# First w_up tile split into high and low parts at the 96th exponential and scaling of the attention instead of the 48th

## What is computed

```python
o_nsa = nsa_attention(...)            # 8 heads, blocks: compressed, selected, window
o_fox = forgetting_attention(...)     # 8 heads, causal with decay
merged = sigmoid(gm_nsa) * (o_nsa @ w_up_nsa) + sigmoid(gm_fox) * (o_fox @ w_up_fox)
return merged @ w_o
```

## Time and profile before

| | |
|---|---|
| time, median of 3 runs | 2453.43 us (2452.48 to 2454.91) |
| profiled execution, its own time | 2450.02 us |
| its span in the trace | 2448.1 us |
| PE busy | 95% of the span |
| DVE, ACT, POOL busy | 57%, 44%, 51% |
| granted TensorE clock, mean | 0.98 of full speed |

### The profile page before, as it was taken

How to read it: one execution, slowest core, us unless ns; L and a number is a source line. 1 busy time by engine, 2 the same in 40 slices (tenths; PEclk the granted TensorE clock), 3 DMA queues, 4 the chain that set the end, 5 groups by cost and what they waited for, 6 DMA issues and landing times. The chain is left out here.

```text
span 2448.1 us, 30080 instructions
## 1 busy us (share of the span) xinstructions
PE 2316.3 (95%) x10920; PEld 1884.8 (77%) x10920; DVE 1385.6 (57%) x1664; ACT 1088.6 (44%) x2060; POOL 1249.8 (51%) x967
## 2 busy tenths in 40 slices
PE   4999999999999899999799999999789999999997
PEld 2788888888877777788677877777578888888885
DVE  5846555266557755742588888575463323225554
ACT  4533333323445443333688888423543333323332
POOL 3454444445564555444557545355745555435473
PEclk7999999999999999999899999999999999999998
DMA  6155544265451433343803046323212222245362
GB/s 254 59 185 176 189 174 160 75 227 168 151 168 48 142 120 128 143 170 129 248 14 88 18 110 173 105 93 130 94 53 85 83 82 94 73 169 175 116 188 88
DMA packets 128946, 314.98 MB, mean 129 GB/s; under 512 B 13408, under 2 KB 34016, under 8 KB 128800
## 3 DMA queue, kind: packets, MB, share of 16 engines
q1 hardware_dynamic: 127824, 310.76, 38.5%
q10 hardware_dynamic: 976, 2.29, 0.4%
HBM read 241.51 MB, written 69.34 MB: 127 GB/s over the span
## 5 line engine op out<-in xcount | busy, mean ns | idle before, releaser
L1635 POOL TENSOR_TENSOR r_z<-f_main,r_z 128x512 fp32r<-128x512 f32 x254 | 353.4, 1394 | 394.3 <-ACT r_z L1031 394.1
L2536 PE MATMUL ps<-r_main,r_z 128*128 128x512 f32 x1232 | 483.7, 393 | 21.4 <-issue 13.4
L2537 PE MATMUL ps<-r_main,r_z 128*128 128x512 f32 x1232 | 481.7, 391 | 0.0
L2538 PE MATMUL ps<-r_main,r_z 128*128 128x512 f32 x1232 | 481.4, 391 | 0.0
L1641 POOL TENSOR_TENSOR r_main<-f_main,r_main 128x1024 fp32r<-128x1024 f32 x88 | 217.0, 2469 | 221.3 <-ACT r_main L1072 221.3
L2536 PEld LDWEIGHTS ps<-r_main,r_z 128*128 128x128 f32 x1232 | 232.8, 189 | 71.3 <-issue 23.0
L2512 PE MATMUL ps<-r_main 128*128 128x512 f32 x688 | 269.0, 391 | 3.4 <-DVE r_main L1998 3.4
L2538 PEld LDWEIGHTS ps<-r_main,r_z 128*128 128x128 f32 x1232 | 232.8, 189 | 48.9
L2537 PEld LDWEIGHTS ps<-r_main,r_z 128*128 128x128 f32 x1232 | 232.9, 189 | 48.7 <-issue 0.2
L2514 PE MATMUL ps<-r_main 128*128 128x512 f32 x688 | 267.8, 389 | 0.0
L2513 PE MATMUL ps<-r_main 128*128 128x512 f32 x688 | 267.7, 389 | 0.0
(11 more groups left out here) (309 smaller groups left out, 4626.8 us busy)
## 6 DMA issues: line engine op xcount, KB each, us to landing
f_main<-in_wd SPq DMA_DIRECT2D x88, 512.0 KB, 3.7
f_main<-in_w_ada SPq DMA_DIRECT2D x56, 512.0 KB, 5.1
act_d<-f_main SPq DMA_DIRECT2D x88, 256.0 KB, 2.0
f_main<-act_d SPq DMA_DIRECT2D x88, 256.0 KB, 3.8
f_main<-in_wg SPq DMA_DIRECT2D x20, 1024.0 KB, 5.0
f_main<-in_wu SPq DMA_DIRECT2D x20, 1024.0 KB, 5.1
f_main<-in_wmix SPq DMA_DIRECT2D x18, 1024.0 KB, 5.3
r_main<-qk_hi_d SPq DMA_DIRECT2D x40, 256.0 KB, 7.1
```

The costliest lines, as they stand in the source:

```text
L1635: pool.tensor_tensor(prod_lo_t[slot], source_of(g), prod_hi_t[slot].bitcast(F32), ALU.subtract).then_inc(s["wl"], 1)
L2536: pe.matmul(out, wh, hi, start=start, stop=False, skip_group_check=True)
L2537: pe.matmul(out, wh, lo, start=False, stop=False, skip_group_check=True)
L2538: return pe.matmul(out, wl, hi, start=False, stop=stop, skip_group_check=True)
```

## The change

One constant is added. `up_high(0)` is placed behind E95 in place of E47, and `up_low(0)` behind C95 in place of C47. The waits inside both, the tiles and every transfer stay as they are, and so does the order on PE, DVE and SP.

```diff
+UP_FIRST = 95
...
             for kind, k in stages(A_ACT, E=8):
                 if kind == "E":
                     exp(k)
-                    if k == 47:
+                    if k == UP_FIRST:
                         up_high(0)
...
                     if k == 12 * NT + 11:
                         constant_rows(at)
-                    if k == 47:
+                    if k == UP_FIRST:
                         up_low(0)
```

## The result

Over 20 runs of each, the changed kernel takes 2448.25 us (2444.33 to 2453.04) and the kernel before 2453.03 us (2449.9 to 2455.67). The ratio is 0.998 with an interval of 0.9974 to 0.9986, so 3.4 to 6.4 us are won, 4.8 by the medians. The forecast was 2447.6, in a range of 2443.5 to 2450.5.

A forecast was written before the change was run, and what follows sets the result against it. PE, busy 95%, was taken as bound, its gap caused by ACT's cast waiting for w_up. 9.4 - 0.5 - 2.5 - 0 = 6.4 us won; 2453.4 - 6.4 + 0.6 = 2447.6 us, range 2443.5 to 2450.5.

The forecast's parts named there:

- The bound and the wait that takes over: ACT's cast waits 11.95 us for w_up, idling PE 12.30; next G2 waits some 6 us for group 0's store.
- Term 1: At S31 on PE: start moves from 1225.63 to 1216.2, limited by the store's landing; 9.4 us won.
- term 2: w_up and store transfers slow from 416 to 370 GB/s beside busy engines for about 5 us; 0.5 us lost.
- Term 3: PE runs 5.1 us at low clock after its new gap ahead of S31; 2.5 us lost.
- The lower bound of 1.9: Least loss to PE's low clock after the new gap, in us; the upper bound was 3.2.
- Term 4: At E95 and C95: ACT's cast and POOL's subtraction are covered by idle time or slack; cost 0.
- The sum: 9.4 - 0.5 - 2.5 = 6.4 us off the profiled execution, giving 2443.6; 2447.6 us for the median.
- The correction for the long half clock: Profile of before had 6.4 us low clock, 5.1 expected in other runs; 0.6 us of gain not in the median.
- (a): At G2: the store overtakes the w_up loads and G2 finds it landed; 16 us won, 2437; chance 0.05.
- (b): At G2: same wait but less won, by later landing, longer low clock or pipeline refill; 4.0 us, 2449.4; chance 0.26.
- (c): Slower: store lands beyond 1224.0, so the pair is pure cost at its new place; 2456; chance 0.03.
- (d): Nothing changes, because w_up is waited for elsewhere as well; chance 0.03.

The follow-up runs named there:

- E95: Not a run: ACT's exponential at the 96th step, behind which the changed kernel places the cast; its last record there is at 1288.85.
- E47: Not a run: ACT's exponential at the 48th step, behind which the kernel before has the cast; last record 1201.68 before, 1203.59 in the changed kernel.
- store0_first: Changed kernel with the store of output group 0 queued on SP ahead of the eight w_up loads; 2437.51 us against 2452.06 for the kernel before.
- store0_first_at47: Kernel before, pair at its old place, with the group 0 store queued ahead of the w_up loads; 2452.17 us against 2452.06.
- E96: Not a run: ACT's exponential after E95, whose start ends the measured stage; 1294.49 before, 1289.99 in the changed kernel.
- low_only: Changed kernel with ACT's cast back behind E47, so only POOL's half of the pair is moved; 2451.36 us against 2452.06 for the kernel before.
- tile0_alone_at47: Kernel before, pair at the 48th step, w_up tile 0 on its own semaphore so the cast waits for that load only; 2443.41 us against 2451.94.
- tile0_and_store0: Kernel before with w_up tile 0 on its own semaphore and the group 0 store ahead of the loads; 2445.48 us against 2452.04.
- store0_in_middle: Changed kernel with the group 0 store queued behind four of the eight w_up loads; 2435.78 us against 2452.04 for the kernel before.
- loads_behind_3: Changed kernel with the eight w_up loads queued behind the stores of groups 0, 1 and 2; 2439.67 us against 2452.06 for the kernel before.
- changed_again: The changed kernel repeated unaltered beside other runs of the kernel before; 2448.38 us against 2451.94, ratio 0.9982.
- at53: Changed kernel with the pair behind E53 and C53 in place of E95 and C95; 2448.29 us against 2451.94 for the kernel before.
- at191: Changed kernel with the pair behind E191 and C191 in place of E95 and C95; 2447.41 us against 2451.94 for the kernel before.

## Why the prediction was right

**The bound and the wait that takes over.** The forecast said that G2 would be held by the store of group 0, which lands behind the w_up loads, and that this is late next. The trace shows 7.11 us of it, where "some 6 us" was said, and `store0_first` and `store0_first_at47` show that it is this wait and that it only counts once the cast's is gone. The times of day that the prediction gives for the changed kernel, such as 1216.7 for S31, are all exceeded by about 1.9 us, because E47 itself came 1.9 us later in this execution; the distances from E47 hold.

**Term 1 and 2 (9.4 won, 0.5 lost).** From E47's last record to S31 it took 1225.63 - 1201.68 = 24.0 us before and 1218.68 - 1203.59 = 15.1 after, 8.9 us less; 9.4 - 0.5 is 8.9. The store landed 1217.1 - 1203.59 = 13.5 us after that record, against 1214.6 - 1201.68 = 12.9 before, 0.6 us later; from the landing to S31 it took the 1.6 us of the reckoning. So the 0.5 of term 2 has the right size, but that is luck: its reason is not what the trace shows. The transfers did not slow down to 370 GB/s beside busy engines. They ran at 418 and 403 GB/s from 1206 to 1210, with PE, ACT and POOL at work, which is what they had in the old gap (416). In the repetition G2 started 0.6 us later still. Why the store lands 0.6 to 1.2 us later than before stays open.

**Term 3 (2.5 lost to the clock).** The stage as a whole won 6.4 us of these 8.9, so 2.5 were lost behind S31, with 5.3 us at half clock where 5.1 were reckoned. That it is the clock is shown by the same stretch of work in all profiled executions. Between S31 and E96 no engine waits for a transfer in any of them, and the time goes by the half clock alone (in us; the half clock is reckoned from stretches of 2 us):

| kernel | E47's last record to S31 | half clock behind S31 | S31 to E96 |
|---|---|---|---|
| before | 24.0 | 0 | 68.9 |
| `store0_first_at47` | 24.2 | 0 | 68.9 |
| `low_only` | 22.1 | 0 | 68.9 |
| `tile0_alone_at47` | 15.0 | 0 | 68.9 |
| `tile0_and_store0` | 14.2 | 0 | 68.9 |
| `store0_in_middle` | 9.9 | 0 | 68.9 |
| `store0_first`, `loads_behind_3` | 8.7 | 0 | 68.9 |
| changed kernel | 15.1 | 5.3 | 71.3 |
| `changed_again` | 15.7 | 5.4 | 71.4 |
| `at53` | 17.4 | 3.5 | 70.5 |
| `at191` | 14.7 | 3.2 | 70.3 |

A microsecond at half clock costs a little under half a microsecond, as term 3 has it. That 5.1 was so near is partly luck: `at191`, which has the changed kernel's order in this stage, had 3.2. The lower bound of 1.9 is also a little off. It takes the 3.8 us from PE's resuming at 788.77 to full clock as all half clock, but the matmul at 788.77 took 0.47 us, as matmuls do at full clock.

**Term 4 (nothing for the pair).** From E95's last record to E96 it takes 1289.99 - 1288.85 = 1.14 us, and it took 1294.49 - 1293.35 = 1.14 before; the cast fits into the idle time. C96 starts 3.4 us after E96, against 1296.31 - 1294.49 = 1.8 before: 1.6 us later, where 1.7 was said. Ahead of 1322.71 the idle time is again 3.80 us, and that step is 4.5 us earlier than in the earlier trace rows, as E96 is. POOL's subtraction was expected at about 1289 and starts at 1291.05, right behind C95 and without a wait; the 2 us are those by which E47 was later. Between 1300 and 1325, where T74 lies, no gap of PE is longer than 0.31 us. `low_only` (for POOL's half) and `at191` confirm that the pair costs nothing that can be told.

**The sum.** 6.4 us were forecast against the profiled execution and 5.8 against the median. For a single execution the forecast of 2443.6 did not hold: the profiled one took 2449.13, since the later start and the part behind E96 took 1.9 and 3.6 us of the 6.4 back. That is scatter that the text left out of this number. The stage measured 6.4 and, in the repetition, 5.8 less than before; by the medians 4.8 us were won, in an interval of 3.4 to 6.4. The 1.0 us between 5.8 and 4.8 is inside that interval. With 4.8 us the effect lies at the 0.2% that the text took as the border of what can be told; by the interval it is a gain. The correction for the long half clock in the profile of before was in the right direction: after their gaps `low_only` and `store0_first_at47`, in which ACT waits for w_up as before, had 3.4 and 5.1 us of it in place of 6.4.

**The rivals.** (a), the overtaking store, did not happen in the sense that counts: one half of the store landed about 1 us ahead of the last load, but the other half 0.7 us behind it, 10.9 us after its issue. But the size of (a) was nearly right, and it could be had by moving the store. (b), the same wait with less won, is not excluded by the median of 4.8, which lies between its 4.0 and the forecast's 5.8; in the two profiles the landing was 0.6 and 1.2 us late, not 1.6, and the half clock 5.3 and 5.4 us long, not 6.4. (c) and (d) did not happen.

The prediction did not see that, where G2 has to wait, a short wait ahead of it can be better than none: `tile0_alone_at47` keeps the pair where it was and beats the change: a stage of 83.9 us against 86.4 and 87.0.

## What to carry to other kernels

When a wait for a transfer is taken off an engine, look down its queue for the next wait on the same DMA queue, and reckon the gain to that landing and not to zero; here 12 us of waiting gave 5 us, and moving one 256 KB store ahead of 4 MB of loads gave 10 more. Where PE must be idle once, the half clock that follows is part of the price of the gap (2.5 us here), unless it falls into time that would be waited out anyway. And with gaps in later stages whose cost differs by some microseconds from run to run, compare the stage by marks at both its ends, and the whole by many runs.

## What was not expected of the hardware

The half clock added nothing where it fell into time that would have been waited out anyway: with a gap of 3.46 us ahead of it, PE ran at 0.50 from 1206 to 1212, S31 came as long after E47 as in the changed kernel (15.0 and 15.1 us), and the stage was 2.5 to 3.1 us shorter than with the gap first and the half clock after it.

One half of a store landed about 1 us ahead of a load that had been issued before it (1215.2 and 1216.4), and the other half 0.7 us behind that load (1217.1).

With much queued, a single issue can hold SP for long: in the kernel before that of the first w_up load took 8.6 us and each of the next seven 0.4 us, and in `store0_first` that of the store's first transfer took 7.9 us. Transfers that stand behind it in SP's order are issued that much later. What SP waits for in these times isn't shown.

The code from E96 to the end is all but the same in these kernels, and it took between 1151.7 us (`store0_in_middle`) and 1158.1 us (`store0_first_at47`) in the profiled executions. In the pair of before and after, 2.8 us of their difference of 3.6 lie between one gap of PE in the second SwiGLU block and the next load of SP, where the one resumed at full clock after 2.68 us and the other at half clock after 4.76 us.
